# Second step of the side modulations: pairs joined in one product of 128 rows, gate sums spread in rounded parts

## The reference, cut to what matters

```python
def _adaln(c, w, b):
    return jnp.dot(jax.nn.silu(c), w) + b
...
        shift, scale, gate = jnp.split(_adaln(c, p['mod_w_a'][i], p['mod_b_a'][i]), 3, axis=-1)
        h = _rmsnorm(x, p['ln_pre_a'][i]) * (1.0 + scale[:, None, :]) + shift[:, None, :]
...
        x = x + gate[:, None, :] * _rmsnorm(y, p['ln_post_a'][i])
    kv_shift, kv_scale = jnp.split(_adaln(c, p['mod_w_kv'], p['mod_b_kv']), 2, axis=-1)
```

## Time and profile before

| what | value |
|---|---|
| median of 3 runs | 936.82 us |
| the profiled execution | 938.4 us |
| its span, first to last instruction | 936.6 us |
| PE busy | 888.2 us, 95% of the span |
| DVE busy | 476.9 us, 51% |
| ACT busy | 409.0 us, 44% |
| share of PE in the chain that ended last | 84% |

### The profile page before, as it was taken

The page is one execution under the profiler, slowest core; times in us unless marked ns, Lnnn a source line. Parts: engine busy times, 40 slices in busy tenths (PEclk is TensorE's granted clock), DMA queues, the critical chain, the costliest instruction groups (busy, mean ns, idle before and its releaser), DMA issues.

```text
span 936.6 us, 15205 instructions
## 1 busy us (share of the span) xinstructions
PE 888.2 (95%) x5846; PEld 688.4 (74%) x5846; DVE 476.9 (51%) x893; ACT 409.0 (44%) x891; POOL 29.8 (3%) x79
## 2 busy tenths in 40 slices
PE   5899999999999999997999799999989999998896
PEld 4677666777677777665878688888867887876685
DVE  4442334222387776567437524342376565477735
ACT  5341221212266666567336412342246666566622
POOL 0000000000000000110000000000000000022000
PEclk9999999999999999998999999999999999999999
DMA  9965645764321202695233124243221020396522
GB/s 307 369 223 191 240 142 188 278 251 158 122 105 45 71 21 82 237 331 206 68 113 113 64 69 153 98 148 122 68 68 46 24 93 6 136 328 245 188 89 112
DMA packets 72915, 138.56 MB, mean 148 GB/s; under 512 B 4369, under 2 KB 31377, under 8 KB 72721
## 3 DMA queue, kind: packets, MB, share of 16 engines
q1 hardware_dynamic: 69360, 126.59, 39.3%
q0 software_dynamic: 3200, 11.01, 3.2%
q10 hardware_dynamic: 288, 0.04, 0.0%
HBM read 121.37 MB, written 16.25 MB: 147 GB/s over the span
## 4 chain that ended last, share of the span: by engine, by line
PE 84%; DVE 6%; ACT 4%; DMA 3%; issue 2%; SPq 1%; POOL 0%; ACTq 0%; DVEq 0%
PE bank L1644 20%; PE bank L1646 19%; PE bank L1645 19%; PE bank L1711 3%; PE bank L1687 2%; PE bank L1804 2%; PE bank L1958 2%; PE bank L1823 2%; PE bank L1815 2%; PE bank L1974 2%; DMA arena<-in_mod_w_a 1%; PE bank L1883 1%; PE bank L1862 1%; PE bank L1639 1%; PE bank L1659 1%
## 5 line engine op out<-in xcount | busy, mean ns | idle before, releaser
L1644 PE MATMUL bank<-w_parts,h_parts 128*128 128x512 f32 x640 | 258.2, 404 | 12.8 <-DVE w_parts L1175 6.3
L1646 PE MATMUL bank<-w_parts,h_parts 128*128 128x512 f32 x640 | 251.0, 392 | 0.0
L1645 PE MATMUL bank<-w_parts,h_parts 128*128 128x512 f32 x640 | 250.8, 392 | 0.0
L1644 PEld LDWEIGHTS bank<-w_parts,h_parts 128*128 128x128 f32 x640 | 121.0, 189 | 48.4 <-issue 17.0
L759 ACT ACTIVATE w_parts<-arena 128x1024 fp32r<-128x1024 f32 x64 | 67.3, 1053 | 180.4 <-PE bank L1646 168.4
L1646 PEld LDWEIGHTS bank<-w_parts,h_parts 128*128 128x128 f32 x640 | 121.0, 189 | 26.5
L1175 DVE TENSOR_TENSOR w_parts<-arena,w_parts 128x1024 fp32r<-128x1024 f32 x64 | 78.1, 1222 | 118.4 <-ACT w_parts L759 118.0
L1645 PEld LDWEIGHTS bank<-w_parts,h_parts 128*128 128x128 f32 x640 | 121.3, 189 | 23.1
L1644 PE MATMUL bank<-h_parts,w_parts 128*128 128x320 f32 x256 | 90.1, 352 | 1.6 <-ACT arena L876 0.9
L1646 PE MATMUL bank<-h_parts,w_parts 128*128 128x320 f32 x256 | 79.6, 311 | 0.0
L1645 PE MATMUL bank<-h_parts,w_parts 128*128 128x320 f32 x256 | 79.4, 310 | 0.0
(11 more groups left out here) (165 smaller groups left out, 1194.7 us busy)
## 6 DMA issues: line engine op xcount, KB each, us to landing
arena<-in_w_in_a SPq DMA_DIRECT2D x32, 512.0 KB, 4.2
arena<-in_mod_w_b SPq DMA_DIRECT2D x12, 1024.0 KB, 6.3
arena<-in_mod_w_a SPq DMA_DIRECT2D x10, 1024.0 KB, 10.2
arena<-in_mod_w_kv SPq DMA_DIRECT2D x8, 1024.0 KB, 6.4
arena<-in_cache_a_k SPq DMA_DIRECT2D x16, 512.0 KB, 6.3
arena<-in_cache_a_v SPq DMA_DIRECT2D x16, 512.0 KB, 5.1
arena<-in_w_kv_b SPq DMA_DIRECT2D x16, 512.0 KB, 3.8
arena<-in_w_in_b SPq DMA_DIRECT2D x16, 512.0 KB, 3.9
```

The lines of the kernel that those rows point to most:

```text
L1644: mm(out, ah, wh, start=start, stop=False)
L1645: mm(out, ah, wl, start=False, stop=False)
L1646: return mm(out, al, wh, start=False, stop=stop)
```

## The change

The four pairs of shift and scale pieces get one task for a pair in place of two. Its four products use all 128 rows, with a selector of 18 columns (C_SE2, 9 for each half of the rows), so that a product gives 128 columns of both pieces; DVE takes both pieces in one pass. The slots 15, 17, 20 and the second task of slot 22 are left empty.

The gate sums are read in two operations: a rounded high part (fp32r) and the difference as a low part. Each gate task then is two fp32r products, for the high and the low part, accumulated in the bank, with a rounded copy of the selection matrices (`spread`, made once by DVE) as weights. The first gate task waits for that copy too (s_spread).

```diff
-C_N = C_PAIR + 2 * P
+C_SE2 = C_PAIR + 2 * P
+C_N = C_SE2 + 2 * ROWS
...
+        t[(p % 32 == r) & (p < HD), C_SE2 + r] = 1.0
+        t[(p % 32 == r) & (p >= HD), C_SE2 + ROWS + r] = 1.0
...
-            tasks += [(pos, r) for r in range(1 if mods[m][2] < 4 else 2)]
+            if mods[m][2] >= 4:
+                tasks += [(pos, 0), (pos, 1)]
+            elif pos < NF or (pos - NF) % 2 == 0:
+                tasks.append((pos, 0))
...
+        def msum_low(ci):
+
+            return (sub(X_r, 18, NC), sub(RA_r, 18, NC))[ci]
+
+        def msum_high(ci):
+
+            return (sub(X_r, 16, NC), sub(RA_r, 16, NC))[ci]
+
+        spread = sub(RA_r, 14, 2 * P)
...
             def read_partial(m):
...
+                if m in (NF, NF + 1):
+                    link(nc.vector.tensor_copy(msum_high(m - NF), ps[5][:, 0:w]))
+                    nc.vector.tensor_tensor(msum_low(m - NF), ps[5][:, 0:w], msum_high(m - NF).bitcast(F32), ALU.subtract)\
+                        .then_inc(s_msum, 1)
+                    return
...
             def finish_task(n):
...
                 elif c < 4:
                     vi = {"a": 0, "kv": 2, "b": 4}[group] + c // 2
-                    k = slice(4 * (c % 2), 4 * (c % 2) + 4)
-                    dst = modT[:, vi, k, :]
-                    bias = biasT[:, vi, k].unsqueeze(2).to_broadcast([P, 4, ROWS])
-                    src = mod_bank(n)[:, 0:4 * ROWS].rearrange("p (k r) -> p k r", k=4)
+                    dst = modT[:, vi, :, :]
+                    split = dst.rearrange("p (h f) r -> p h f r", h=2)
+                    bias = biasT[:, vi, :].rearrange("p (h f) -> p h f", h=2).unsqueeze(3).to_broadcast([P, 2, 4, ROWS])
+                    src = mod_bank(n)[:, 0:KT * ROWS].rearrange("p (f h r) -> p h f r", f=4, h=2)
...
+            nc.vector.tensor_copy(spread, const[:, C_EXP:C_EXP + 2 * P]).then_inc(s_spread, 1)
             nc.vector.tensor_copy(maskb[:, :], maskf).then_inc(s_maskb, 1)
...
             def second(n):
...
-                r0 = HD * ((pos - NF) % 2)
-                rows = slice(0, P) if pos < NF else slice(r0, r0 + HD)
-                if c < 4:
-                    for f in range(2 * (PIECES[pos][1] - PIECES[pos][0]) if pos < NF else 4):
-                        last = mm(bank[:, ROWS * f:ROWS * (f + 1)], m[rows, P * f:P * (f + 1)],
-                                  const[rows, C_SEL:C_SEL + ROWS], start=True, stop=True)
+                if n == NF:
+                    pe.wait_ge(s_spread, 1)
+                if pos < NF:
+                    for f in range(2 * (PIECES[pos][1] - PIECES[pos][0])):
+                        last = mm(bank[:, ROWS * f:ROWS * (f + 1)], m[:, P * f:P * (f + 1)],
+                                  const[:, C_SEL:C_SEL + ROWS], start=True, stop=True)
+                elif c < 4:
+                    for f in range(4):
+                        last = mm(bank[:, 2 * ROWS * f:2 * ROWS * (f + 1)], m[:, P * f:P * (f + 1)],
+                                  const[:, C_SE2:C_SE2 + 2 * ROWS], start=True, stop=True)
                 else:
-                    c0 = (C_EXP, C_EXS)[r]
-                    last = mm(bank[:, :], const[rows, c0:c0 + P], m[rows], start=True, stop=True)
+                    r0 = HD * ((pos - NF) % 2)
+                    rows = slice(r0, r0 + HD)
+                    for a, part in enumerate((msum_high, msum_low)):
+                        last = mm(bank[:, :], spread[rows, P * r:P * (r + 1)], part((pos - NF) // 2)[rows],
+                                  start=a == 0, stop=a == 1)
```

More of the change, by code:

```diff
@@ L101, in sem @@
             return ctx.enter_context(nc.semaphore(name))
+        with nc.sbuf_tensor("arena_rounded", [P, 141 * KB], F32R) as rounded:
+            pass
         arena = sb("arena", [P, 141 * KB])
@@ L112, in build @@
         X, RA, RB, RC, RD, KN = (region(20) for _ in range(6))
+        X_r, RA_r = (rounded[:, 20 * KB * n:20 * KB * (n + 1)] for n in range(2))
         WR, RH = region(16), region(5)
@@ L301, in build @@
         s_x = [sem(f"x_in{t}") for t in range(TT)]
+        s_spread = sem("spread_rounded")
         s_maskb, s_silu_c, s_cz, s_lam, s_lamx = (sem(n) for n in (
@@ L1150, in finish_task @@
                     vi = {"a": 0, "kv": 2, "b": 4}[group] + c // 2
-                    k = slice(4 * (c % 2), 4 * (c % 2) + 4)
-                    dst = modT[:, vi, k, :]
-                    bias = biasT[:, vi, k].unsqueeze(2).to_broadcast([P, 4, ROWS])
-                    src = mod_bank(n)[:, 0:4 * ROWS].rearrange("p (k r) -> p k r", k=4)
+                    dst = modT[:, vi, :, :]
+                    split = dst.rearrange("p (h f) r -> p h f r", h=2)
+                    bias = biasT[:, vi, :].rearrange("p (h f) -> p h f", h=2).unsqueeze(3).to_broadcast([P, 2, 4, ROWS])
+                    src = mod_bank(n)[:, 0:KT * ROWS].rearrange("p (f h r) -> p h f r", f=4, h=2)
                     if vi % 2 == 0:
-                        nc.vector.tensor_tensor(dst, src, bias, ALU.add).then_inc(s_mdone, 1)
+                        nc.vector.tensor_tensor(split, src, bias, ALU.add).then_inc(s_mdone, 1)
                     else:
-                        link(nc.vector.tensor_tensor(dst, src, bias, ALU.add))
-                        ln = lnT[:, vi // 2, k].unsqueeze(2).to_broadcast([P, 4, ROWS])
+                        link(nc.vector.tensor_tensor(split, src, bias, ALU.add))
+                        ln = lnT[:, vi // 2, :].unsqueeze(2).to_broadcast([P, KT, ROWS])
                         link(nc.vector.tensor_scalar(dst, dst, 1.0, None, ALU.add))
```

## The result

The changed kernel takes 930.31 us in the median of five executions (929.54 to 933.06). The kernel before, run beside it, takes 938.46 (five executions, 936.59 to 939.71). The ratio is 0.9922 with a 95% interval of 0.99 to 0.9944. It is faster, as forecast, but 930.31 lies above the forecast of 927.7 and just outside its range of 925.1 to 929.8. Of the 2.6 us between forecast and result, 1.6 are the kernel before itself (938.46 over these five executions, 936.82 over the first three of them, which the sum was set against), and 1.0 is a smaller gain: 8.15 us by the medians for 9.1 forecast. The interval alone does not exclude a gain of 9.1 us (a ratio of 0.9903); that the gain fell short is read from the stage.

The account below looks back on a forecast made before the run. PE was taken to bound the kernel, busy for all 195.00 us of the stage from 60 to 255 us. Columns 5.4 plus gates 3.7 made 9.1 us off 936.82: 927.7 us, range 925.1 to 929.8.

Parts of the forecast that it names:

- what bounds the stage: From 60 to 255 us PE is busy for all 195.00 us, so a microsecond saved there comes off the end.
- The column tasks: Shift and scale pieces: four tasks gone, 4.5 us, four with 128 rows, 1.0, less 0.1 for 18 columns: 5.4 us.
- late batches: Rival: side weights land after 11.3 us, not 6.7, PE waits, up to all 9.1 us given back: 936.8 us; chance 0.04.
- more than one pass: Rival: rounded gate products run as two instructions each, like fp32, 8.4 us more: 939.8 us, slower; chance 0.03.
- exposed load: Rival: the second product's weight load lies bare in each of 8 gate tasks, 0.9 us less saved: 928.6 us; chance 0.15.
- free borders: Rival: changes between 64 and 128 rows cost nothing between rounded products; gates give 6.3 us, total 925.1 us; chance 0.12.
- the gate term: The 8 gate tasks, each as two rounded products, save 8 x 0.46 = 3.7 us of PE time, between 3.0 and 6.3.
- two streams of 0.23 go: 0.46 for a task: In a gate task the 512 columns stream twice instead of four times, loads and tile changes unchanged: 0.46 us saved.
- my bounds of 0.37 and 0.79: Saving per gate task in us: 0.37 if each product costs 0.34, 0.79 if the two follow without any extra.
- the step on DVE: The second operation of 0.7 us in each of two gate-sum reads on DVE was claimed to cost PE nothing.
- the uncovered price as 1.6 for two reads: If DVE's two longer gate-sum reads were not covered, they would cost 2 x 0.8 = 1.6 us.
- the base: The kernel before's median of 936.82 us, from which the 9.1 us gain was subtracted to give 927.7 us.

Follow-up runs that it names:

- the fill: Kernel before plus 10 useless products in PE's idle time in the opening: 938.36 us, ratio 0.9989 (0.998 to 0.9998) to the kernel before.

## Why the prediction was right or wrong

**Right:** what bounds the stage. PE's time saved there is time saved at the end: 8.06 us of stage, 8.15 us by the medians. The column tasks were costed at 5.4 and gave 5.60, four gone and four shorter; 18 columns cost what 9 do (0.80 and 0.81 us for the eight instructions). No batch came late, and the products of rounded parts are one instruction each, so the rivals of the late batches and of more than one pass fall. The exposed load falls too, though not by its sign: with 0.66 us a task came out nearer to the 0.68 of that case than to the 0.6 of the forecast. What decides is that on 128 rows, with both loads still to the same rows, the two products take 0.45, and that the 0.34 of the first product stands behind a change of tile on 128 rows as well. The Trainium skill, "TensorE: Matmul & The Clock Gate", Part 3 (The mechanism), has a sentence by which a load overlaps products in flight only in another row group, and this trace does not agree: two loads to the same 64 rows lie within 0.30 us, beside the first product. The same section of the Trainium skill also lets a load go ahead into a background weight buffer; whether that is what happens here, no run shows. The free borders also fall: 0.31 ahead and 0.34 behind stay with rounded products on both sides, and go with 128 rows. "TensorEngine Tiling (Array Packing)", Key Properties, of the Trainium skill has a drain at a change of tiling mode, and here the trace agrees: 0.31 with the change of tile, 0.23 without.

**Wrong, first:** the gate term. The step "two streams of 0.23 go: 0.46 for a task" was too large; a task gave 0.39, and the term 3.1 in place of 3.7. I had priced a stream by the distance of two whole products, 0.23; each of the two instructions became only about 0.20 shorter by the stream that it lost (0.54 to 0.34, 0.51 to 0.32). Whether a stream inside an instruction takes less than that distance, or the loads and tile changes, which the step kept "as they are", cost a little more with short products, was not tested. The 0.39 lay between my bounds of 0.37 and 0.79, close to the lower.

**Wrong, second:** the step on DVE, "So nothing". I named as queued behind the read of the sums only the low part of the next slot's weights, which has a slot of slack, and counted idle time over the stage. Behind it stands also DVE's copy of the transposes, whose bank PE wants 0.7 us after that copy began, just as it ends. The list of waits of the kernel before had the sign of it, in a row of PE's weight loads, where I had looked at those of PE:

```profile
PEld bank L1711 <- DVE arena L1240: 0.3, 1, 0.3
```

The load of these transposes already waited for the copy, so the copy had no slack to give. The price of this one operation is 0.70 to 0.78 us in three kernels, and 0.84 in the one with gate tasks of 128 rows. I had written the uncovered price as 1.6 for two reads; only the one in slot 8 is uncovered, as no transposes run beside the first.

**Wrong, third:** the base. The sum was set against 936.82 from three runs, two of them low (936.59 and 936.82); the four comparisons since have medians of 938.46 to 939.42. I took a microsecond for the spread of the runs, and that was too little. Set against 938.46, 9.1 us would have given 929.4, 0.9 under the measured 930.31, and the range moved by as much would have held it: the base, more than the two terms, put the result outside. Why those two executions were so fast stays open. The later comparisons ran on three chips, and which chip the first one ran on is not known. The clock in the opening is not enough of a reason: the profiled execution of the kernel before has no fall of the clock there and took 938.4, and with the fill none of 11 executions came under 937.52.

Together the stage gives 5.6 + 3.1 - 0.7 = 8.0 us, for 9.1 forecast.

## What to carry to other kernels

An operation added to an engine that is half idle is free only if every instruction queued behind it in program order has more slack than its length, so list them all to the next wait of the bottleneck engine; a shared buffer that this engine must empty is the one to look for. Where small products stand between large ones, padding them to the tile of their neighbours can be worth nearly as much as making them cheaper: 0.40 us for a gate task between projections and 2.36 us over all eight, beside the 3.1 of the rounded parts. And before a forecast is set against a median of three, look whether the kernel's runs fall in groups.

## What the runs showed of the hardware that was not expected

A product of 128 rows, half of them zeros, takes 0.23 us like any other and leaves no border, while a task of two products on 64 rows costs 0.85 us in place of 0.45, about 0.2 us for each of its two borders. A weight load for the same 64 rows goes on beside the product ahead of it: two loads lie within 0.30 us, and the second product starts 0.34 after the first. An idle time of PE of 2.55 us in the opening was followed by a fall to the lower clock level, at a cost of 1.6 us, in six of nine profiles, and with 2.39 us of it filled by useless products in none of four. That makes the idle time the likely cause; four profiles are few.
